# Sixteen and eight extra TensorE products around attention's first head, into an unread PSUM bank

## The chip, the core and the metric

The kernel runs on one core of a Trainium2 chip. The metric is the device time of one execution in microseconds (us), the median of several runs. Stretches are given in us from the start of the profiled execution's span.

## The reference, cut to what matters

Two layers of a decoder trunk on x of 512 tokens by 1024 features in float32. Each layer is a SwiGLU half step, a mixer and a second SwiGLU half step. The mixer of the second layer is stick-breaking attention with 16 heads of 64 features, strictly causal; the change lies there.

```python
q = rms_norm(to_heads(q), q_g); k = rms_norm(to_heads(k), k_g)
z = jnp.einsum('bhqd,bhkd->bhqk', qb, kf)            # logits
neg_log_keep = jnp.where(mask, jax.nn.softplus(z), 0.0)
rcs = lax.cumsum(neg_log_keep, axis=3, reverse=True)  # suffix sums
a = jnp.where(mask, jnp.exp(jax.nn.log_sigmoid(z) - suffix), 0.0)
return jnp.einsum('bhqk,bhkd->bhqd', a, vf)
```

## The kernel before

The trunk is one program with an instruction stream written out for each engine; the engines meet at semaphores that count. Float32 products are made of three products of split operands, high by high, high by low and low by high (`triple`, lines 1323 to 1325), in the type float32r. Weights stream in slabs through `raw`, are split by ScalarE and VectorE into `w`, and are multiplied by TensorE; q, k and v come out of twelve such slabs.

After the last slab TensorE spreads the last four head norms over 128 rows (`head_spread`, blocks 12 to 15, lines 1593 and 1594, products of 32 rows by 512 columns). VectorE multiplies them into q and k (`normalise`, line 1224) and signals `qkn_done`. For heads 0 and 1 VectorE rounds q and k (`split_qk`, lines 1257 and 1258) and GpSimd subtracts to get the low parts (`split_low`, lines 540 and 543), which signals `qklo_done`. Each later pair of heads is split in the same way, one pair ahead: pair 1 (heads 2 and 3) behind `softplus` of head 0 in VectorE's stream.

On TensorE each head has these blocks. `logits(t, p)` adds the mask (line 1646, products of `con`, 128 columns) and the products of q and k, 64 rows each, for key blocks 1, 3, 2 (p = 0) and 0 (p = 1). `suffix(t, p)` (line 1664) makes the suffix sums from the softplus of the logits, split into `sp_hi` and `sp_lo`, ten instructions for each part and head, 128 rows. `values(c2)` (line 1678) makes the output of a pair of heads. In between, ScalarE takes the absolute value, Exp and Ln (lines 784, 788, 790) and later Exp of the weights (line 771); VectorE adds and splits (lines 1263, 1270, 1275, 1277). The order on TensorE is written out by hand: logits of head t+1, part p, then suffix of head t, part p; `values(c2)` comes after the suffix sums of head 2*c2+2.

`con` holds four constant 128 by 128 matrices: the identity, the mask (0 and -1e30), a triangle of -1, and all -1; it has been in place since 1412 us. PSUM has eight banks; logits use banks 0 to 5, `values` banks 6 and 7. Bank 7 is last read before this by `normalise(13)` and is first written again by `values(1)`, with start set.

Of the kernel before, what the change touches and what calls it, by code (L numbers as in the profile page):

```python
# [29 lines left out]
KD = D // P  # L30
# [60 lines left out]
def trunk(nc, x_in, up_in, down_in, mix_in, ada_in, vec_in, dw_in, dwb_in, con_in, ind_in, sel_in, out):  # L91
    ctx = ExitStack()
    with ctx:
# [3 lines left out]
        def sem(name):  # L97
            return ctx.enter_context(nc.semaphore(name))
# [35 lines left out]
        with ExitStack() as scope:  # L134
            def ov(name, shape, dt=F32):
                return scope.enter_context(nc.sbuf_tensor(name, shape, dt))
# [20 lines left out]
        with ExitStack() as scope:  # L157
# [8 lines left out]
            con = ov("con", [P, 4, P], F32R)  # L166
# [16 lines left out]
        ps = ctx.enter_context(nc.psum_tensor("ps", [P, 8, S], F32))  # L183
# [85 lines left out]
        conr_done = sem("conr_done")  # L269
# [8 lines left out]
        qkn_done = sem("qkn_done")  # L278
# [34 lines left out]
        def spread_bank(b):  # L313

            return down_ps[b % 2] if b < KD or b >= 14 else ps[:, 6 + b % 2, :]
# [1004 lines left out]
        def _(pe):  # L1320
            def triple(dst, a_hi_, a_lo_, b_hi_, b_lo_, start, stop):

                pe.matmul(dst, a_hi_, b_hi_, start=start, stop=False, skip_group_check=True)  # L1323
                pe.matmul(dst, a_hi_, b_lo_, start=False, stop=False, skip_group_check=True)  # L1324
                return pe.matmul(dst, a_lo_, b_hi_, start=False, stop=stop, skip_group_check=True)  # L1325
# [261 lines left out]
            def head_spread(b):  # L1587

                pe.wait_ge(y_done, 2 * (b // KD) + 2)
                if 2 <= b < 14:  # L1590
                    pe.wait_ge(qkn_done, b - 1)
                w = sel[:, b % KD, :]
                pe.matmul(spread_bank(b), w, y_hi[:, :], start=True, stop=False)
                pe.matmul(spread_bank(b), w, y_lo[:, :], start=False, stop=True).then_inc(bc_done, 1)

            for s in range(12):
                n = N_QKV + s
# [28 lines left out]
            def span(base, c, q0):  # L1626

                return slice(base + at_key[c] + q0 - P * c, base + at_key[c] + S - P * c)

            def logits(t, p):  # L1630


                base = 3 * S * (t % 2)
                blocks = ((1, 3, 2), (0,))[p]
                c2, half = t // 2, t % 2
                rows = slice(HD * half, HD * half + HD)
                pe.wait_ge(qklo_done, 2 * c2 + 2)
                if t == 1:
                    pe.wait_ge(qkn_done, 2 * KD)
                if t == 0:  # L1640
                    pe.wait_ge(conr_done, 2)
                    pe.wait_ge(vf_done, 8)
                if t >= 2:
                    pe.wait_ge(a_done, 2 * (t - 2) + p + 1)
                for c in blocks:
                    pe.matmul(zps[:, base + at_key[c]:base + at_key[c] + P], con[:, 0, :], con[:, 1, :],
                              start=(c != 3), stop=False, skip_group_check=True)
                for c in blocks:
                    keys = slice(P * c, P * (c + 1))
                    seen = slice(P * c, S)  # L1650
                    last = triple(zps[:, span(base, c, P * c)], qk_s[rows, c2 % 2, 2, keys],
                                  qk_s[rows, c2 % 2, 3, keys], qk_s[rows, c2 % 2, 0, seen],
                                  qk_s[rows, c2 % 2, 1, seen], False, False)
                last.then_inc(z_done, 1)

            def suffix(t, p):

                base = 3 * S * (t % 2)
                blocks = ((1, 2, 3), (0,))[p]
                for part in (sp_hi, sp_lo):  # L1660
                    pe.wait_ge(sphi_done if part is sp_hi else splo_done, 2 * t + p + 1)
                    for c in blocks:
                        for later in range(c, 4):
                            last = pe.matmul(zps[:, span(base, c, P * later)],  # L1664
                                             con[:, 2 if later == c else 3, :],
                                             part[:, span(0, later, P * later)],
                                             start=False, stop=(part is sp_lo), skip_group_check=True)
                last.then_inc(cum_done, 1)

            def values(c2):  # L1670

                pe.wait_ge(a_done, 4 * c2 + 4)
                if c2 >= 2:
                    pe.wait_ge(o_done, c2 - 1)
                for c in range(4):
                    for half in range(2):
                        cols = slice(P * c2 + HD * half, P * c2 + HD * (half + 1))
                        last = pe.matmul(ps[HD * half:HD * half + HD, 6 + c2 % 2, P * c:S], v_f[:, c, cols],  # L1678
                                         a_f[:, (2 * c2 + half) % 4, span(0, c, P * c)], start=(c == 0), stop=(c == 3),
                                         skip_group_check=True)  # L1680
                last.then_inc(av_done, 1)

            head_spread(14)
            head_spread(15)
            for p in range(2):
                logits(0, p)
            for t in range(HEADS):
                for p in range(2):
                    if t + 1 < HEADS:
                        logits(t + 1, p)  # L1690
                    suffix(t, p)
                if t % 2 == 0 and t >= 2:
                    values(t // 2 - 1)
# [74 lines left out]
```

## Time and profile before

| what | value |
|---|---|
| median of 3 runs | 2105.23 us (2102.99 to 2106.54) |
| the profiled execution's own time | 2103.05 us |
| its span | 2101.3 us, 1.75 us less than its time |
| mean granted TensorE clock | 0.983 of full speed |

Full speed is 2.4 GHz; a granted clock of 0.50 is 1.2 GHz. In views of one engine's instructions the duration of a product overlaps that of the next; what a product costs in a row of them is the distance between two starts. In the stretches view the first number is the stretch's length, then come the busy time (and number of instructions) of each engine, the granted clock, the share of DMA and its rate.

### The profile page before, as it was taken

To read this page: it belongs to the slowest core of one execution; us is meant where nothing else is said; L and a number is where in the kernel's file an instruction comes from. 1 tells how busy PE (TensorE), PEld (TensorE's weight loads), DVE (VectorE), ACT (ScalarE), POOL (GpSimd) and SP (SyncE) were. 2 spreads that over 40 slices of the span, in tenths; PEclk is the share of its full clock that TensorE was granted. 3 is DMA by queue.
4 is the path that set the end of the run, shared out by engine and by line. 5 is a ranking of instruction groups with operands and counts; after the bars stand their busy time and mean duration, and the time that the engine had idled before them with its cause. 6 is when DMAs were issued, how large, how long until landed. Compare 5 with 4: busy or idle time off the path is not lost.

```text
span 2101.3 us, 24264 instructions
## 1 busy us (share of the span) xinstructions
PE 2043.3 (97%) x9512; PEld 1654.3 (79%) x9512; DVE 1113.2 (53%) x1326; ACT 677.2 (32%) x760; POOL 183.8 (9%) x129
## 2 busy tenths in 40 slices
PE   5999999989999999999999999999999999999999
PEld 5888888766567888888788888887787777888887
DVE  7555553588977555533655433364446855333322
ACT  2423232241244232222423222242136744222211
POOL 1100000111302000001100000110001110000000
PEclk9999999999989999999999999999978999999999
DMA  8445443334413444432354422232200032222222
GB/s 326 177 162 197 185 170 143 143 108 138 133 67 125 184 190 180 169 117 98 118 189 189 160 88 84 97 103 99 80 1 1 1 120 81 100 100 91 78 96 95
DMA packets 45414, 261.80 MB, mean 125 GB/s; under 512 B 6416, under 2 KB 7056, under 8 KB 20528
## 3 DMA queue, kind: packets, MB, share of 16 engines
q1 hardware_dynamic: 42288, 256.84, 33.3%
q10 hardware_dynamic: 3072, 4.23, 0.8%
q8 instruction: 35, 0.57, 0.1%
q14 instruction: 19, 0.16, 0.0%
HBM read 250.49 MB, written 2.10 MB: 120 GB/s over the span
## 4 chain that ended last, share of the span: by engine, by line
PE 85%; DVE 6%; DMA 3%; issue 3%; ACT 2%; POOL 1%; SPq 0%; DVEq 0%; POOLq 0%; ACTq 0%
PE ps L1323 25%; PE ps L1325 25%; PE ps L1324 25%; PE ps L1664 3%; DVE w L811 1%; DMA raw<-down_d 1%; PE ps L1344 1%; PE ps L1546 1%; DMA stage<-ada_d 1%; PE ps L1678 1%; DVE act_tmp L824 1%; DVE ada_acc L824 1%; PE ps L1584 1%; ACT w L560 1%; PE ps L1437 1%
## 5 line engine op out<-in xcount | busy, mean ns | idle before, releaser
L1323 PE MATMUL ps<-h_hi,w 128*128 128x512 f32 x1648 | 649.9, 394 | 8.2 <-DVE w L976 6.8
L1325 PE MATMUL ps<-h_hi,w 128*128 128x512 f32 x1648 | 648.9, 394 | 0.0
L1324 PE MATMUL ps<-h_lo,w 128*128 128x512 f32 x1648 | 646.2, 392 | 0.0
L1323 PEld LDWEIGHTS ps<-h_hi,w 128*128 128x128 f32 x1648 | 310.4, 188 | 84.6 <-DVE w L976 8.1
L1324 PEld LDWEIGHTS ps<-h_lo,w 128*128 128x128 f32 x1648 | 310.4, 188 | 68.6
L1325 PEld LDWEIGHTS ps<-h_hi,w 128*128 128x128 f32 x1648 | 310.5, 188 | 66.5
L811 DVE TENSOR_TENSOR w<-raw,w 128x1408 fp32r<-128x1408 f32 (+1 forms) x100 | 186.4, 1864 | 239.3 <-ACT w L560 239.2
L560 ACT ACTIVATE w<-raw 128x1408 fp32r<-128x1408 f32 (+1 forms) x100 | 157.0, 1570 | 443.9 <-PE ps L1325 377.0
L1323 PE MATMUL ps<-g_hi,w 128*128 128x512 f32 x704 | 274.6, 390 | 4.3 <-DVE w L811 4.3
L1324 PE MATMUL ps<-g_lo,w 128*128 128x512 f32 x704 | 273.9, 389 | 0.0
L1325 PE MATMUL ps<-g_hi,w 128*128 128x512 f32 x704 | 273.9, 389 | 0.0
L976 DVE TENSOR_TENSOR w<-raw,w 128x2048 fp32r<-128x2048 f32 x80 | 183.4, 2292 | 79.7 <-ACT w L625 79.7
L970 DVE TENSOR_TENSOR act_tmp<-act_tmp,ps 128x512 f32<-128x512 f32 x85 | 58.4, 688 | 314.9 <-ACT act_tmp L620 314.9
L620 ACT ACTIVATE act_tmp<-ps 128x512 f32<-128x512 f32 x85 | 50.8, 598 | 445.6 <-PE ps L1325 441.2
L824 DVE SCALAR_TENSOR_TENSOR ada_acc<-ada_raw,e_col,ada_acc 128x512 f32<-128x512 f32 x224 | 171.4, 765 | 8.3 <-DMA ada_raw<-ada_d 1.5
L1323 PEld LDWEIGHTS ps<-g_hi,w 128*128 128x128 f32 x704 | 132.2, 188 | 32.8 <-DVE w L811 5.7
L1325 PEld LDWEIGHTS ps<-g_hi,w 128*128 128x128 f32 x704 | 132.2, 188 | 27.6
L1324 PEld LDWEIGHTS ps<-g_lo,w 128*128 128x128 f32 x704 | 132.2, 188 | 27.4
L625 ACT ACTIVATE w<-raw 128x2048 fp32r<-128x2048 f32 x80 | 152.0, 1900 | 0.0
L972 DVE TENSOR_TENSOR g_lo<-act_tmp,g_hi 128x512 f32 (+1 forms) x85 | 58.9, 692 | 75.5 <-ACT g_hi L622 75.5
L953 DVE SCALAR_TENSOR_TENSOR x<-ps,gt,x 128x512 f32<-128x512 f32 x48 | 35.7, 748 | 114.1 <-PE ps L1325 114.1
L478 POOL TENSOR_TENSOR parts<-ada_acc,parts 128x512 fp32r<-128x512 f32 x27 | 35.0, 1297 | 577.4 <-ACT parts L611 577.4
(210 smaller groups left out, 1925.3 us busy)
## 6 DMA issues: line engine op xcount, KB each, us to landing
raw<-up_d SPq DMA_DIRECT2D x88, 1024.0 KB, 6.3
ada_raw<-ada_d SPq DMA_DIRECT2D x64, 1024.0 KB, 4.8
raw<-down_d SPq DMA_DIRECT2D x64, 704.0 KB, 4.1
raw<-mix_d SPq DMA_DIRECT2D x28, 1024.0 KB, 4.8
stage<-ada_d SPq DMA_DIRECT2D x12, 1024.0 KB, 13.0
u_blk<-u SPq DMA_DIRECT2D x64, 64.5 KB, 2.1
u_blk<-u ACTq DMA_DIRECT2D x64, 64.5 KB, 2.1
x<-x_t_d SPq DMA_DIRECT2D x2, 1024.0 KB, 18.0
```

Of the source, the lines that this page charges most:

```text
L560: act.activation(wsp[n % 2][:, 0, 0:cols], raw[n % 2][:, 0:cols], ACT.Copy).then_inc(hi_done, 1)
L620: act.activation(tmp, pair[s][0], ACT.Silu).then_inc(silu_done, 1)
L625: act.activation(wsp[s][:, 0, :], raw[s][:, :], ACT.Copy).then_inc(hi_done, 1)
L811: dve.tensor_tensor(wsp[n % 2][:, 1, 0:cols], raw[n % 2][:, 0:cols], f32(wsp[n % 2][:, 0, 0:cols]), ALU.subtract) \
L824: dve.scalar_tensor_tensor(out=acc, in0=buf[:, k, :], scalar=w, in1=acc, op0=ALU.mult, op1=ALU.add).then_inc(ada_step, 1)
L970: dve.tensor_tensor(tmp, tmp, pair[s][1], ALU.mult).then_inc(g_full, 1)
L972: dve.tensor_tensor(g_lo[:, 2 * i + s, :], tmp, f32(g_hi[:, 2 * i + s, :]), ALU.subtract).then_inc(g_done, 1)
L976: dve.tensor_tensor(wsp[s][:, 1, :], raw[s][:, :], f32(wsp[s][:, 0, :]), ALU.subtract) \
L1323: pe.matmul(dst, a_hi_, b_hi_, start=start, stop=False, skip_group_check=True)
L1324: pe.matmul(dst, a_hi_, b_lo_, start=False, stop=False, skip_group_check=True)
L1325: return pe.matmul(dst, a_lo_, b_hi_, start=False, stop=stop, skip_group_check=True)
L1664: last = pe.matmul(zps[:, span(base, c, P * later)], con[:, 2 if later == c else 3, :], part[:, span(0, later, P * later)], start=False, s ...
```

## The change

A helper `keep_clock(n)` issues n products of `con`'s identity with all four matrices of `con` (128 rows, 512 columns, float32r) into PSUM bank 7, each with start and stop set. It waits first until `con` is in place and until 14 blocks of q and k are normalised. Sixteen products come after the last two `head_spread` and ahead of `logits(0, 0)`; eight more come after `logits(1, 0)` and ahead of `suffix(0, 0)`. Nothing reads them, and nothing waits for them by a semaphore.

```diff
+            def keep_clock(n):
+
+                pe.wait_ge(conr_done, 1)
+                pe.wait_ge(qkn_done, 2 * KD - 2)
+                for _ in range(n):
+                    pe.matmul(ps[:, 7, :], con[:, 0, :], con[:, :, :].rearrange("p c n -> p (c n)"), start=True,
+                              stop=True, skip_group_check=True)
+
             head_spread(14)
             head_spread(15)
+            keep_clock(16)
             for p in range(2):
                 logits(0, p)
             for t in range(HEADS):
                 for p in range(2):
                     if t + 1 < HEADS:
                         logits(t + 1, p)
+                    if t == 0 and p == 0:
+                        keep_clock(8)
                     suffix(t, p)
```

## Rows read from the trace of the kernel before

**Rows 1.** The page: the span, and the granted clock in 40 slices.

```profile
span 2101.3 us, 24264 instructions
PEclk9999999999989999999999999999978999999999
```

**Rows 2.** Stretches of attention, with the granted clock behind POOL's busy time.

```profile
1548.55:1551.97 3.42, 2.67 (x14) 1.80 (x12) 2.10 (x5) 2.37 (x3) 0.28 (x1) 1.00 0.00 0
1551.97:1554.34 2.37, 0.00 (x1) 0.00 (x1) 1.29 (x2) 0.00 (x0) 2.32 (x2) 0.50 0.00 0
...
1563.06:1573.52 10.46, 10.46 (x37) 9.06 (x36) 6.89 (x13) 5.36 (x7) 2.62 (x2) 0.50 0.00 0
...
1591.28:1592.93 1.65, 1.65 (x5) 0.53 (x6) 1.44 (x3) 0.60 (x1) 0.00 (x0) 0.50 0.00 0
...
1616.22:1680.00 63.78, 63.78 (x402) 50.39 (x403) 51.77 (x80) 49.19 (x68) 10.58 (x8) 1.00 0.00 1
```

**Rows 3.** Instructions in order of time between the last slab and the first logits.

```profile
1549.87 1.41 DVE L1224 SCALAR_TENSOR_TENSOR qk<-qk,vec,ps 128x512 f32<-128x512 f32 x2 [7.28 <-PE ps L1594]
...
1550.83 0.39 PE L1594 MATMUL ps<-y_lo,sel 32*128 32x512 f32 x1
...
1554.34 0.90 PE L1646 MATMUL ps<-con 128*128 128x128 f32 x3 [3.12 <-POOL qk_s L543]
```

**Rows 4.** The chain of waits through attention: start, length, engine and line.

```profile
1563.13 2.96 PE ps L1664 x12
...
1570.42 0.64 PE ps L1646 x3
...
1591.35 3.10 PE ps L1678 x16
1594.45 0.48 PE ps L1646 x3
...
1596.34 1.64 PE ps L1664 x12
...
1598.98 1.43 PE ps L1664 x8
1600.41 0.34 PE ps L1646 x3
...
1602.16 1.64 PE ps L1664 x12
...
1606.22 2.30 PE ps L1678 x16
```

**Rows 5.** Instructions on ScalarE, VectorE and GpSimd behind head 0's logits.

```profile
1557.88 0.81 ACT L784 ACTIVATE sp_abs<-ps 128x768 f32<-128x768 f32 x1 [6.29 <-PE ps L1325]
...
1561.55 0.56 DVE L1275 CAST sp_hi<-sp_abs 128x768 fp32r<-128x768 f32 x1
...
1566.65 1.27 POOL L543 TENSOR_TENSOR qk_s<-qk,qk_s 128x512 fp32r<-128x512 f32 x1
```

**Rows 6.** TensorE's products of 128 rows by 512 columns, at each clock.

```profile
665.99 0.40 PE L1325 MATMUL ps<-h_hi,w 128*128 128x512 f32 x1
666.22 0.40 PE L1323 MATMUL ps<-h_hi,w 128*128 128x512 f32 x1
...
1043.59 0.63 PE L1324 MATMUL ps<-h_lo,w 128*128 128x512 f32 x1
1044.02 0.63 PE L1325 MATMUL ps<-h_hi,w 128*128 128x512 f32 x1
```

**Rows 7.** Stretches around two waits of TensorE outside attention.

```profile
663.15:665.41 2.26, 0.00 (x0) 0.00 (x0) 2.26 (x2) 0.60 (x1) 0.00 (x0) 1.00 0.00 0
665.41:668.00 2.59, 2.59 (x11) 2.15 (x12) 2.48 (x4) 0.00 (x0) 0.00 (x0) 1.00 0.00 0
...
1040.89:1043.16 2.27, 0.00 (x0) 0.00 (x1) 2.27 (x2) 0.60 (x1) 0.00 (x0) 1.00 0.00 0
...
1043.38:1046.79 3.41, 3.41 (x9) 2.62 (x9) 2.97 (x5) 0.29 (x1) 0.00 (x0) 0.50 0.00 0
```

## The prediction

> **What bounds the kernel now.** I read the page first. TensorE is the long engine, and of the 40 slices of granted clock three fall below 9 tenths: the 12th, near 600 us, and the two that begin with the first heads of attention, at 7 and 8 tenths [rows 1]. The stretches view dates the fall in attention: full clock up to 1551.97, 0.50 from there, still 0.50 in the stretch that ends at 1592.93, and 1.00 all the way from 1616 to 1680 [rows 2]. So the clock lies at its lower level (1.2 GHz) for 1592.93 - 1551.97 = 41 us, and TensorE is busy in nearly all of it.
>
> What the engine did before the fall is in [rows 2, 3]: the last products were eight spreads of 32 rows (the last starts at 1550.83), then nothing; the clock was down about 0.8 us after the last product, and the first logits started only at 1554.34, released by GpSimd's low part of k, after 3.12 us of idle. What it did before the rise: suffix sums of 128 rows, and straight behind them the first `values` from 1591.28 [rows 2]. The mixture of logits (64 rows) and suffix sums did not bring the clock back in four heads' work, and the same mixture later ran at full clock for 64 us without a fall. The state is thus inherited: what the first head finds decides what the first three or four heads cost.
>
> The chain of waits shows that this stage is TensorE's at either clock. At full clock a head without `values` takes 1602.16 - 1596.34 = 5.82 us [rows 4]: suffix part 0 takes 1.64, logits part 1 the 1.00 between 1597.98 and 1598.98, suffix part 1 takes 1.43, logits part 0 takes 1602.16 - 1600.41 = 1.75. At half clock the same head takes 10.46 [rows 2], with TensorE busy throughout.
>
> **The change part by part.** It removes nothing; it adds 24 products and a wait, all on TensorE. The wait on `con` is long met; the one on 14 normalised blocks ends with the second instruction of VectorE's pair that starts at 1549.87 and lasts 1.41, at 1551.28, against 1551.22 for TensorE's own last product [rows 3]: it costs some 0.1 us, covered by the idle time. Behind it are only the logits, which wait until 1554.34 anyway. No DMA is moved: none of SP's loads is issued in this stage but those that wait for the last suffix sums, and they come earlier by as much as those do.
>
> *Sixteen products.* 128 by 512 products follow each other at 0.23 us at full clock (665.99 to 666.22) and at 0.43 at half (1043.59 to 1044.02) [rows 6]. 16 x 0.23 = 3.7 us from 1551.3 end at 1555.0: 3.0 us lie in the idle time, 0.65 us on the path. If the clock stays at full, `logits(0, 0)` takes 1.75 instead of the 3.4 that it took from 1554.34 to ScalarE's start behind it at 1557.88 [rows 3, 5], and ends at 1556.8, 1.0 us earlier than before. `logits(0, 1)` and `logits(1, 0)` then take 1.00 + 1.75 and end at 1559.55.
>
> *Eight products.* Head 0's softplus runs on ScalarE and VectorE, whose times don't follow TensorE's clock: `sp_hi` was done at 1561.55 + 0.56 = 1562.11, and is done 1.0 earlier, at 1561.1 [rows 5]. 8 x 0.23 = 1.85 us from 1559.55 end at 1561.4: 1.55 us hidden in that wait, 0.3 us on the path. `suffix(0, 0)` starts at 1561.5 instead of 1563.1 [rows 4], 1.6 us ahead.
>
> *The next wait.* suffix, logits, suffix at full clock are 1.64 + 1.00 + 1.43 = 4.07 us, to 1565.6. `logits(2, 0)` needs the low parts of pair 1, and those come from GpSimd: done before at 1566.65 + 1.27 = 1567.92 [rows 5], hidden then, since the slow TensorE came to them only at 1570.42 [rows 4]. They too move by 1.0 only, to 1566.95. So a new wait of about 1.4 us opens, and `logits(2, 0)` starts at 1567.0, 3.4 us ahead. I have found no third wait: the later pairs have the 2.30 us of a `values` between split and use, and the full-clock heads ran without one.
>
> *The rest of the low stage.* From 1570.42 to the first `values` at 1591.35 are two heads, 20.93 us; at full clock 2 x 5.82 = 11.64, a gain of 9.3. The first `values` took 3.10, partly slow, against 2.30 [rows 4]: 0.8. Sum, if the clock holds: 3.4 + 9.3 + 0.8 = 13.5 us, and everything behind shifts with it. The profiled execution took 2103.05 us, so it would be 2089.5; it lies 2.2 us under the median of the runs, so for the median 2105.23 - 13.5 = 2091.7.
>
> *Does the clock hold?* No row shows products of `con` in an idle stretch, nor the clock's answer to them. Bounds: all 13.5, or a loss (rival 3). I take that they count as other products of 128 rows do, since the mask products and suffix sums with `con` as operand ran at full clock [rows 2, 4]. The weak points are two stretches behind them. One is 4.5 us of logits alone (1555.0 to 1559.55), 64 rows in most products. The other is the new 1.4 us wait followed by 1.75 us of logits. For waits the trace has this: 2.26 us at 663 left the clock at full, 2.27 us at 1041 was followed by 3.41 us at 0.50 [rows 7], with dense products on both sides each time; a third one of 2.27 at 1754 went like the second. So a wait of one length goes either way, about as the moment falls, and here a shorter wait has thinner work behind it. I call it even.
>
> The Trainium skill, TensorE: Matmul & The Clock Gate, section Why this matters for your kernels, asks for no long idle gaps between bursts of products and names no shorter ones as a danger; by that the wait of 1.4 us would be harmless and the sum would be the full gain. The trace agrees only in part: the clock was down 0.8 us after TensorE stopped at 1551.2 [rows 2, 3], behind products of 32 rows.
>
> **The rivals.**
>
> 1. *The clock falls at the new wait* (chance 0.28). For it: two of the three waits in [rows 7] and the thin logits behind it. Against it: it is shorter than all three. Then the clock falls at some 1567 to 1569, the mixture does not bring it back, as it did not before, and `values` does. From 1567.0 the two heads cost about 20.2 (the first 0.8 us still at full pace) and `values` 3.1, to 1590.3 instead of 1594.45: 4.1 us gained, 2101.1.
>
> 2. *The clock falls in the logits ahead of the first suffix sums and does not return* (0.10). Then the first two logits blocks are fast, to 1557.8, `logits(1, 0)` takes some 3.2 and ends at 1561.0, and the eight products take 8 x 0.43 = 3.4, to 1564.4: 1.3 us later than 1563.1, with all that follows as before: 2106.6, no change to be measured. Against it: eight dense products at half clock are what has gone before the rises in the trace, so this ends more likely in a short dip and a total near the forecast; I count that under the forecast.
>
> 3. *The products don't hold the clock at all; slower* (0.09). Constants into an unread bank may not count as work. The clock then falls at 1551.97 as before. Three products run at full pace; 13 x 0.43 = 5.6 us reach to 1557.6, 3.2 us behind 1554.34. `logits(1, 0)` ends 3.2 us later, `sp_hi` has been there since 1565.3, so all of 8 x 0.43 = 3.4 us adds on. Together 6.6: 2111.8. It decides as soon as the clock is at 0.50 ahead of the first logits. Against it: the wait that thinned the work is filled with full-height products from 1551.3 on.
>
> The change does what it says in each of them but the last, in which 24 products run for nothing.
>
> **How the numbers follow.** The forecast, clock kept or lost for a few us only: 0.53, 2091.7, its own range 2089 to 2095 (the 13.5 by 1 us for the waits that I placed by hand, the median's own scatter of 2, and one fall like that at 1043 more or less, 3.41 us at half clock, 1.7 us). The range for all: the first rival has to be in, so 2089 to 2103.5; out are rivals 2 and 3 (0.19). About 0.2% (4.2 us) is what a measurement of this kernel tells from no change. Faster by more: 0.53 and two thirds of the first rival, which lies at that bound: 0.72. Within: the other third and the second rival, 0.19. Slower: 0.09. If executions differ among themselves, some at 2092 and some at 2101, the median takes the more frequent.
>
> **What the profile after would show.** Sixteen starts 0.23 us apart from 1551.3, granted clock 1.00 through 1552 to 1555; the first logits' release no longer GpSimd's; `suffix(0, 0)` near 1561.5; a wait of 1 to 1.5 us at line 1646 ahead of head 2, released by GpSimd's line 543; the first `values` near 1578.6 and the last suffix sums 13 us ahead; mean clock near 0.993. A clock of 0.50 from about 1568 to 1590 means the first rival; starts 0.43 apart among the sixteen mean the third. The prediction would also be wrong if heads 1 and 2 at full clock wait for ScalarE or VectorE where I let them take 5.82 us.

## The result and the profile after

The changed kernel takes 2092.65 us (median of 8 runs, 2089.35 to 2099.13) against 2104.99 for the kernel before (8 runs, 2102.99 to 2108.84): ratio 0.9943, 95% interval 0.9932 to 0.9954, so 12 us faster. The profiled execution took 2091.8 us with a span of 2090.0, 11.3 us less than the span before.

The page shows that no slice in attention is under 9 tenths of the clock any more, where the 30th and 31st stood at 7 and 8 [rows 1]:

```profile
span 2090.0 us, 24314 instructions
...
PEclk9999999999989999999999999999999999999999
```

The stretches view of attention after the change, with the granted clock behind POOL's busy time (the lines of [rows 2]):

```profile
1551.63:1555.53 3.90, 3.90 (x18) 3.25 (x19) 1.84 (x4) 0.17 (x1) 2.65 (x2) 1.00 0.00 0
1555.53:1558.36 2.83, 2.83 (x17) 2.14 (x16) 0.00 (x0) 1.02 (x2) 0.00 (x0) 1.00 0.00 0
...
1559.20:1561.08 1.88, 1.88 (x10) 1.66 (x8) 1.05 (x2) 1.85 (x3) 0.00 (x0) 0.50 0.00 0
1561.08:1564.79 3.71, 3.71 (x9) 2.94 (x10) 3.61 (x7) 2.64 (x4) 0.05 (x1) 0.50 0.00 0
1564.79:1566.05 1.26, 1.26 (x7) 1.26 (x7) 0.21 (x1) 0.00 (x0) 1.26 (x1) 0.53 0.00 0
1566.05:1571.04 4.99, 4.99 (x32) 4.19 (x31) 3.10 (x5) 2.65 (x4) 1.31 (x2) 1.00 0.00 0
...
1583.27:1670.00 86.73, 86.73 (x546) 69.41 (x547) 68.93 (x104) 66.49 (x92) 13.23 (x10) 1.00 0.00 1
```

The clock is held through the sixteen products and through the first two logits blocks. Then it does fall, at 1559.2, in `logits(1, 0)`, 3.7 us of logits behind the sixteen and with no idle time on TensorE. It is back at full at the start of 1566. So it is at half for 7 us in place of 41.

The chain of waits after, first the part around the first heads and then the first `values` (the lines of [rows 4]; line 1688 is the added product):

```profile
1551.63 3.90 PE ps L1688 x16
1555.53 0.28 PE ps L1646 x3
...
1561.08 3.71 PE ps L1688 x8
1564.79 2.05 PE ps L1664 x12
...
1569.29 0.34 PE ps L1646 x3
...
1580.96 2.30 PE ps L1678 x16
1583.27 0.48 PE ps L1646 x3
```

Head 2's logits start at 1569.29 (1570.42 before), the first `values` at 1580.96 (1591.35 before), and the block behind it at 1583.27 (1594.45 before): 11.2 us, all but 0.1 of what the spans differ by. There is no wait for GpSimd ahead of `logits(2, 0)`; its part was ready at 1567.36, since line 543 ran as this row shows:

```profile
1566.09 1.27 POOL L543 TENSOR_TENSOR qk_s<-qk,qk_s 128x512 fp32r<-128x512 f32 x1
```

### The profile page after: what moved, and what is told of

Its sections match the earlier page's. It is cut to its first block, busy times and chain, and to the rows that moved or that the text cites. A ratio compares the mean times of both kernels' runs of the same rounds, so it can differ in the third digit from the quotient of the medians.

```text
span 2090.0 us, 24314 instructions
## 1 busy us (share of the span) xinstructions
PE 2035.1 (97%) x9536; PEld 1647.7 (79%) x9536; DVE 1113.2 (53%) x1326; ACT 676.3 (32%) x760; POOL 183.6 (9%) x129
## 4 chain that ended last, share of the span: by engine, by line
PE 86%; DVE 7%; DMA 3%; ACT 2%; issue 1%; POOL 1%; SPq 0%; DVEq 0%; POOLq 0%; ACTq 0%
PE ps L1323 26%; PE ps L1324 25%; PE ps L1325 25%; PE ps L1664 2%; DVE w L811 1%; DMA raw<-down_d 1%; PE ps L1344 1%; DMA stage<-ada_d 1%; PE ps L1546 1%; PE ps L1678 1%; DVE act_tmp L824 1%; DVE ada_acc L824 1%; PE ps L1584 1%; ACT w L560 1%; PE ps L1437 1%
```

## The experiments

Nine kernels were run, one of them three times. Medians and numbers of runs, each beside runs of the kernel before on the same chip:

| kernel | median, us | lowest to highest | runs | ratio to before, 95% interval |
|---|---|---|---|---|
| changed kernel (16, then 8) | 2092.65 | 2089.35 to 2099.13 | 8 | 0.9943 (0.9932 to 0.9954) |
| 16 alone | 2104.92 | 2099.58 to 2110.23 | 12 | 1.0004 (0.9995 to 1.0014) |
| 8 alone | 2094.62 | 2092.55 to 2095.21 | 5 | 0.9949 (0.9936 to 0.9962) |
| 16 and 8 of 32 rows | 2112.22 | 2109.54 to 2117.84 | 8 | 1.0036 (1.0021 to 1.0051) |
| 16 and 8, early split | 2092.63 | 2089.82 to 2095.52 | 6 | 0.9943 (0.9929 to 0.9957) |
| 16, 4, 4 | 2099.65 | 2091.59 to 2107.55 | 12 | 0.9973 (0.9961 to 0.9985) |
| 16, 4, 4, early split | 2090.29 | 2089.84 to 2094.91 | 5 | 0.9935 (0.9922 to 0.9947) |
| 13, 4, 3, early split | 2090.61 | 2086.60 to 2092.48 | 5 | 0.9929 (0.9916 to 0.9942) |
| early split alone | 2105.24 | 2104.43 to 2110.93 | 11 | 1.0007 (0.9998 to 1.0016) |
| 16, 4, 4, and 6 in the wait | 2090.63 | 2089.65 to 2093.91 | 6 | 0.9925 (0.9898 to 0.9952) |

The "early split" is explained below. The wide interval of the last row comes from one of the 11 runs of the kernel before beside it, 2121.40 us; the medians alone give 2090.63 / 2104.88 = 0.9932.

The profiles, one for each kernel but three for 16, 4, 4, also give the stretch by itself, free of the scatter elsewhere in the 2100 us: from the first of the last eight spreads to the first product behind the first `values`. It takes 45.3 us in the kernel before, 45.5 with the early split alone, 44.4 with 16 alone, 35.1 with 8 alone, 33.9 in the changed kernel, 52.4 with 32 rows, 32.3 with 16 and 8 and the early split and as much with 16, 4, 4 and the early split, 29.9 with 13, 4, 3, and 33.9 with six more in the wait. The three profiles of 16, 4, 4 have 33.8, 39.8 and 41.5.

### The sixteen alone

```diff
-                    if t == 0 and p == 0:
-                        keep_clock(8)
```

> The sixteen products stay, the eight are left out. My theory (the clock falls in the logits behind the sixteen, as it did at 1559.2 us in the profile of the changed kernel, and only dense products bring it back before the first values product does): the first two logits blocks run fast, then 0.50 until about 1590 us; the time is 1 to 3 us under the kernel before, 2102 to 2104. Rival (the sixteen carry the whole gain, the eight are ballast): 2091 to 2093, mean granted clock 0.99.

2104.92 us, no change. The stretches view of this kernel:

```profile
1553.60:1557.50 3.90, 3.88 (x18) 3.25 (x19) 1.86 (x4) 0.19 (x1) 2.66 (x2) 1.00 0.00 0
1557.50:1560.88 3.38, 3.38 (x21) 2.62 (x20) 0.50 (x1) 1.55 (x2) 0.00 (x0) 1.00 0.00 0
1560.88:1591.88 31.00, 30.68 (x107) 26.41 (x109) 16.88 (x27) 17.74 (x24) 5.26 (x4) 0.50 0.00 1
```

The clock is at 1.00 while the sixteen run and falls at 1560.88, in the logits; nothing ahead of `values` (1591.88) gives it back, and it returns only at 1595.02. In its one profile the stretch is 0.9 us shorter than in the kernel before; the medians, expected at 2102 to 2104, show no gain. The rival, that the sixteen carry the change, falls.

### The eight alone

```diff
-            keep_clock(16)
```

> The eight products stay, the sixteen are left out. My theory (dense products at half clock bring the clock back): it falls at about 1552 us as before, the eight take 3.4 us, and it is back at full at about 1566; suffix(0, 0) starts 3.4 us late, and from there two heads cost 5.8 instead of 10.5 us each: 2094 to 2097. Rival (eight are too few, and the clock stays low until the first values): 3.4 us added, 2108.5.

2094.62 us, as expected: 10 of the 12 us come with eight products. Stretches of this kernel, in whose profile everything from the last spreads on lies 2.4 us later than in the kernel before:

```profile
1554.64:1565.50 10.86, 8.75 (x29) 7.21 (x29) 4.18 (x7) 3.94 (x5) 2.05 (x2) 0.50 0.00 0
1565.50:1568.30 2.80, 2.80 (x8) 2.22 (x8) 2.41 (x6) 2.59 (x3) 0.57 (x1) 0.50 0.00 0
1568.30:1590.00 21.70, 21.70 (x139) 17.96 (x138) 16.12 (x24) 14.89 (x21) 4.70 (x4) 1.00 0.00 1
```

The clock falls in the wait for the first logits as in the kernel before, lies at 0.50 through the logits, and is at 1.00 from 1568.30, 2.8 us after the first of the eight. The same mixture of suffix sums and logits then keeps it.

### The same products with 32 rows

```diff
-                    pe.matmul(ps[:, 7, :], con[:, 0, :], con[:, :, :].rearrange("p c n -> p (c n)"), start=True,
+                    pe.matmul(ps[:, 7, :], con[0:32, 0, :], con[0:32, :, :].rearrange("p c n -> p (c n)"), start=True,
```

> Both groups of products stay in number, columns and place, but each is of 32 rows instead of 128 (the first 32 rows of the constants). TensorE is as long busy by the profile. Theory (products of few rows do not hold the clock, as the eight spreads of 32 rows before the fall in the kernel before): it falls between 1552 and 1555 us, most of the 24 run at half, and it stays low until the first values: 2108 to 2113, slower than before. Rival (any product holds it): 2092, as in the changed kernel.

2112.22 us, 7.5 us slower than before. The order of time on TensorE and the stretches:

```profile
1553.31 6.42 PE L1688 MATMUL ps<-con 32*128 32x512 f32 x16 [0.20 <-DVE qk L1224]
```

```profile
1553.31:1554.18 0.87, 0.87 (x4) 0.73 (x5) 0.87 (x3) 0.17 (x1) 0.60 (x1) 1.00 0.00 0
1554.18:1559.70 5.52, 5.52 (x15) 3.75 (x13) 0.97 (x2) 0.00 (x0) 2.02 (x2) 0.50 0.00 0
1559.70:1600.00 40.30, 40.30 (x132) 33.62 (x132) 17.39 (x27) 19.39 (x25) 5.25 (x4) 0.50 0.00 0
```

The number, the columns and the bank are the same, and by the profile TensorE is just as busy; the clock falls among these products, at 1554.18, without a wait of more than 0.20 us on TensorE since the last slab, and stays down past the eight, to 1601.96. So an engine that the profile calls busy is not enough to hold the clock; the height of the products counts. The cost is near the 6.6 us of the third rival.

### The split of the second pair moved early

```diff
             normalise(15)
+            split_qk(1)
...
-                if t % 2 == 0 and t // 2 + 1 < KD:
+                if t % 2 == 0 and t and t // 2 + 1 < KD:
```

> The changed kernel with the split of the second pair of heads moved ahead of head 0's softplus on VectorE, so that its low parts are there some 7 us before logits(2, 0) can ask for them. Theory (the new wait ahead of logits(2, 0) is what makes the slow executions, as that at 2099.1, and is otherwise hidden by the dip of the clock): median 2090 to 2092.5 and no execution above 2095. Rival (the slow executions come from elsewhere): the scatter stays, one in eight near 2099.

2092.63 us, the changed kernel's time. Two of six, 2095.37 and 2095.52, are a little over the bound that I set; none was near 2099. With one in eight there, six runs don't show that the early split takes such executions away. In the profile the clock still dips in the first heads, for 3.4 us:

```profile
1562.08:1565.50 3.42, 3.42 (x8) 2.67 (x9) 3.28 (x6) 3.32 (x5) 0.00 (x0) 0.50 0.00 0
```

The control has the early split and no products:

> Control: the kernel before with the early split alone and no products. The split was hidden at half clock, so 2104 to 2106, no change. Rival (the split itself is worth time): under 2102.

2105.24 us: the early split alone is worth nothing, as expected.

### Two fours in place of the eight

```diff
                 for p in range(2):
+                    if t == 0 and p == 0:
+                        keep_clock(4)
                     if t + 1 < HEADS:
                         logits(t + 1, p)
                     if t == 0 and p == 0:
-                        keep_clock(8)
+                        keep_clock(4)
```

> The changed kernel with the eight products in two fours, one ahead of logits(1, 0) and one behind it, so that the first heads' logits never run for more than about 2.8 us alone. Theory: the clock no longer falls in the logits at about 1559 us, TensorE is early, and the wait for GpSimd's low part ahead of logits(2, 0), which the dip had hidden, opens with 1.2 to 1.5 us; behind it the clock falls in some of the executions. So executions near 2090 and others 5 to 9 us above them, median not better than the changed kernel's. Rival (such a short wait is harmless to the clock): all near 2090.

2099.65 us, 7 us worse than the changed kernel, from the same number of products with `logits(1, 0)` between the two fours, and the widest scatter of all. In the first profiled execution (2093.1 us) the clock dipped among the sixteen, for 3.41 us, and then stayed at 1.00; the wait was there all the same:

```profile
1572.00 0.55 PE L1646 MATMUL ps<-con 128*128 128x128 f32 x3 [1.27 <-POOL qk_s L543]
```

```profile
1555.42:1558.83 3.41, 3.41 (x10) 2.65 (x9) 1.03 (x2) 0.00 (x0) 2.09 (x2) 0.50 0.00 0
1558.83:1600.00 41.17, 39.90 (x242) 32.10 (x240) 31.22 (x46) 30.08 (x41) 7.93 (x6) 1.00 0.00 1
```

The same kernel was profiled twice more, for a slow execution.

> The kernel with two fours once more, for a profile of a slower execution. Theory: where the mean clock is 0.989 or less, the clock lies at 0.50 from 1567 to 1575 us on until the first values, behind the wait for GpSimd's line 543.

> The same kernel a third time, with the same expectation: a fall behind the wait ahead of logits(2, 0) where the execution is slow, none there where it is near 2092.

They took 2098.15 and 2097.71 us. The first of them, in order of time on TensorE around the wait, then in stretches:

```profile
1565.85 0.79 PE L1664 MATMUL ps<-sp_lo,con 128*128 128x512 f32 x4
...
1567.93 0.55 PE L1646 MATMUL ps<-con 128*128 128x128 f32 x3 [1.28 <-POOL qk_s L543]
```

```profile
1563.00:1570.74 7.74, 6.46 (x42) 5.53 (x41) 7.53 (x13) 4.69 (x7) 2.63 (x2) 1.00 0.01 2
1570.74:1587.80 17.06, 17.06 (x59) 13.86 (x60) 8.15 (x14) 9.77 (x13) 2.63 (x2) 0.50 0.00 0
1587.80:1600.00 12.20, 12.20 (x81) 9.76 (x77) 8.60 (x14) 8.24 (x12) 0.43 (x1) 1.00 0.00 1
```

The clock was at 1.00 through the sixteen and all the logits up to the wait, TensorE came to `logits(2, 0)` 1.28 us too early, and the clock fell 2.8 us after that wait and stayed down until `values`. The second of them also had no dip ahead of the wait, the same wait, and a fall at 1568.20 with the return at 1588.68:

```profile
1565.76 0.55 PE L1646 MATMUL ps<-con 128*128 128x128 f32 x3 [1.29 <-POOL qk_s L543]
```

This is the first rival of the prediction, step for step; it only needed the dip in the first logits out of the way. In these two profiles the stretch given below the table is 6.0 and 7.7 us longer than in the first. The three highest timed runs, 2102.72 to 2107.55, are 10 to 14 us above the first profile, more than such a fall alone explains; they were not profiled. Ten of the twelve timed executions have a mean clock of 0.986 to 0.989, against 0.991 in the changed kernel: 0.003 of 2100 us, twice over since the level is a half, is some 13 us more at half clock.

### The wait taken away, or filled

Two fours with the early split (the two diffs above together):

> The kernel with two fours, and with the split of the second pair moved ahead of head 0's softplus, so that neither the dip nor the wait is left. Theory: clock 1.00 from the sixteen to the end of attention, no wait ahead of logits(2, 0): 2088 to 2090, and little scatter. Rival (other places make the scatter): the same scatter as the changed kernel, median 2091 to 2093.

2090.29 us, just over the 2088 to 2090 expected. From 1556.05 on the clock is at 1.00 to the end of attention, and up to 1600 TensorE waits for nobody:

```profile
1552.64:1556.05 3.41, 3.41 (x10) 2.64 (x9) 2.69 (x4) 0.00 (x0) 3.04 (x3) 0.50 0.00 0
1556.05:1600.00 43.95, 43.95 (x269) 35.86 (x268) 32.32 (x48) 32.75 (x45) 7.00 (x6) 1.00 0.00 1
```

What is left is one stretch of 3.41 us at half among the sixteen themselves, behind the eight spreads of 32 rows; my expectation of 1.00 from the sixteen on was wrong there. The sixteen took 5.49 us with it, against 3.90 in the changed kernel. The same dip is in the first profile of the two fours and in that of the next kernel.

The wait filled with six more products (ahead of `logits(2, 0)`), with the split left late:

```diff
-                    if t == 0 and p == 0:
-                        keep_clock(4)
+                    if t < 2 and p == 0:
+                        keep_clock((4, 6)[t])
                     if t + 1 < HEADS:
```

> The kernel with two fours and the late split, and six more products ahead of logits(2, 0), in the wait of 1.3 us for GpSimd's low part. Theory (the wait with the thin logits behind it is what let the clock fall in most executions of the kernel with two fours): 2089 to 2092, mean clock 0.991 to 0.993, although TensorE has six products more to do. Rival (something else in the split eight lets it fall): near 2099.6 as there.

2090.63 us: six products more in TensorE's stream, and the median is 9 us lower than without them; the two slow profiles of the kernel without them, 2098.15 and 2097.71 us, are from the same chip. All six runs have a mean clock of 0.991 to 0.993, against ten of twelve at 0.989 or less. The rival, that the divided eight lose the clock in some other way, falls. It is these timed runs that show it: the one profile has the dip among the sixteen, as the execution of the two fours that kept its clock at the wait had. Behind that dip it is at full clock:

```profile
1559.61:1600.00 40.39, 40.39 (x239) 32.61 (x240) 30.43 (x46) 30.09 (x41) 7.94 (x6) 1.00 0.00 1
```

With what lay on the path trimmed off (13, 4 and 3 products, early split):

> As the kernel with two fours and the early split, but 13 products instead of 16 and 4 and 3 instead of 4 and 4: what of the products lay on the path is taken off. Theory: 0.7 us less ahead of the first logits and about 0.2 less ahead of the first suffix sums: 0.5 to 1 us under the kernel with 16, 4 and 4, if the clock holds all the same. Rival (three products fewer let the clock fall): 2093 or more.

2090.61 us, without the 0.5 to 1 us expected under 2090.29; its lowest run, 2086.60, is the lowest of all. The profiled execution was at full clock from 1554 to 1669 us, with no dip and no wait, and its stretch, 29.9 us, is the shortest of all:

```profile
1554.00:1600.00 46.00, 45.80 (x276) 37.01 (x275) 36.40 (x55) 33.16 (x46) 10.59 (x8) 1.00 0.00 1
```

Its interval (0.9916 to 0.9942) overlaps those of the two kernels above and the changed kernel's (0.9932 to 0.9954): the three repaired versions are not told apart, and that they beat the changed kernel, by 2 us in the medians, is not shown.

## Why the prediction was right, and where it was not

**The sum.** 13.5 us were predicted for a clock that holds or is lost for a few us only, 2091.7; 12.3 between the medians were measured, and 11.3 between the profiled spans. The sign, the mechanism and the largest term are right: two heads at full clock took 1580.96 - 1569.29 = 11.67 us (11.64 predicted, 20.93 before), and the first `values` took the predicted 2.30. One reading in the sum is off: from 1554.34 to 1557.88 are 3.54 us and not 3.4. That changes nothing, since the start of `logits(0, 1)` was taken as 1557.8 either way.

**The sixteen.** They took 3.90 us (3.7 predicted) and started 0.3 us later than I had put them, with everything ahead shifted by 0.2. The clock was 1.00, and the first two logits blocks took 1558.36 - 1555.53 = 2.83 (2.75 predicted).

**The step that was mis-sized** is the term of 3.4 us for the start of attention, "`suffix(0, 0)` starts at 1561.5 instead of 1563.1". It started at 1564.79. The clock fell at 1559.2, `logits(1, 0)` took 2.72 instead of 1.75, the eight ran at half clock and took 3.71 instead of 1.85, and the first suffix sums took 2.05 instead of 1.64: 3.2 us together. The 3.4 us that I counted up to `logits(2, 0)` came as 1.1. I had named the 4.5 us of logits alone as a weak point and counted a short dip under the forecast, but put no price on it.

**The eight** I costed as filler with 0.3 us on the path. They are what makes the change: without them it gains nothing that the medians show (2104.92), and alone they bring 10 us (2094.62). The second rival, a fall in the logits without a return, is what the sixteen alone do; it was priced at 2106.6 with the eight in the stream, and came to 2104.9 without them.

**The next wait**, 1.4 us for GpSimd's line 543, was not in the profile after. The dip delayed TensorE by 3.2 us, which is more than the wait, and so hid it. That the forecast held is in part luck: the dip, which I left without a price, kept away the wait behind which the clock can fall. With the dip gone it opened with 1.27 to 1.29 us, in each of three profiles, and the clock fell behind it in two; the median, 2099.65, was then outside the 2089 to 2095 that I had given for a clock that holds. One of the changed kernel's eight timed runs took 2099.13 us at a mean clock of 0.988; that this was the same fall fits, but that execution was not profiled, so it is argued and not shown.

**The rule of the Trainium skill** that I weighed, TensorE: Matmul & The Clock Gate, section Why this matters for your kernels, names only long idle gaps between bursts. By it the wait of 1.28 us is harmless; the two profiles near 2098 us say otherwise. The clock was also lost with TensorE busy, in the logits of 64 rows (at 1559.2 in the changed kernel) and in the products of 32 (at 1554.18).

**The third rival**, products that do not hold the clock, is false for 128 rows, and for 32 rows it came about: 7.5 us slower, against the 6.6 worked out for it.

## What to carry to other kernels

When TensorE's clock lies at half over a long busy stretch, look for what started it: a few microseconds of dense full-height products there, even at half clock, can give most of the stretch back, and here eight of them were worth 10 us. Put them behind the thin work that loses the clock, not only ahead of it, and vary the two groups one at a time. Then look for what the faster engine now waits for: here a wait of 1.3 us for another engine, invisible before, cost more than half the gain in most executions until it was taken away or filled.

## What the runs showed of the hardware that I had not expected

Products of 32 rows by 512 columns, issued back to back, did not keep the clock at 2.4 GHz: it went to 1.2 within 0.87 us of the first of sixteen, behind eight others of 32 rows, and the eight that came later did not bring it back. With 128 rows the clock was back at 2.4 GHz 2.8 us after the first of the eight where they stood alone, and 5.0 us after it, in the suffix sums behind them, in the changed kernel. Height alone is not the whole of it: suffix sums of 128 rows, in blocks of up to 2.96 us between the logits, did not bring it back in the kernel before.

One kernel went two ways at one wait: 1.27 us of idle left the clock at full in one profile, and 1.28 and 1.29 us were followed by 17 and 20 us at half in two others. The first had dipped for 3.41 us among the sixteen and the two others had not; whether that decides it, or where in time the wait falls, no run here shows. The timed runs go from 2091.59 to 2107.55, and the first profile alone would have called the kernel good.
